# Block one in one chain, with shared buffers, finer steps and another written-out order

## Time and profile before

| what | us |
|---|---|
| median of 3 runs (lowest, highest) | 1390.18 (1389.88, 1391.13) |
| the profiled execution | 1390.79 |
| its span, first to last instruction | 1388.9 |
| PE busy | 1172.6 |
| DVE, POOL, ACT busy | 725.8, 664.4, 574.2 |

### The profile page before, as it was taken

The page is one execution under the profiler, slowest core; times in us unless marked ns, Lnnn a source line. Parts: engine busy times, 40 slices in busy tenths (PEclk is TensorE's granted clock), DMA queues, the critical chain, the costliest instruction groups (busy, mean ns, idle before and its releaser), DMA issues. The chain is left out here.

```text
span 1388.9 us, 17561 instructions
## 1 busy us (share of the span) xinstructions
PE 1172.6 (84%) x6858; PEld 1027.6 (74%) x6858; DVE 725.8 (52%) x1099; ACT 574.2 (41%) x790; POOL 664.4 (48%) x288
## 2 busy tenths in 40 slices
PE   1999979999758699997999974879999677999864
PEld 0999978898547598997889864768788456887743
DVE  2465475653972456447664486244636622653553
ACT  2452236314542356224531453335457342546622
POOL 2664255524334476335642452568436554734643
PEclk9999999999878899999999987889999887999987
DMA  5553243423232355224432331345324415523420
GB/s 184 171 149 92 67 146 111 118 61 106 66 117 70 120 146 146 82 77 122 136 107 61 91 94 59 106 138 157 109 84 128 135 46 182 154 80 95 148 91 31
DMA packets 84433, 152.17 MB, mean 110 GB/s; under 512 B 10560, under 2 KB 16512, under 8 KB 84224
## 3 DMA queue, kind: packets, MB, share of 16 engines
q1 hardware_dynamic: 84352, 151.06, 36.4%
HBM read 149.99 MB, written 1.05 MB: 109 GB/s over the span
## 5 line engine op out<-in xcount | busy, mean ns | idle before, releaser
L739 POOL TENSOR_TENSOR w_lo<-raw,w_hi 128x1024 fp32r<-128x1024 f32 (+3 forms) x284 | 664.2, 2345 | 702.0 <-ACT w_hi L1156 701.7
L1156 ACT ACTIVATE w_hi<-raw 128x1024 fp32r<-128x1024 f32 (+3 forms) x284 | 287.4, 1017 | 566.3 <-PE bulk L791 446.2
L791 PE MATMUL bulk<-w_hi,hT_hi 128*128 128x512 f32 (+1 forms) x800 | 334.3, 418 | 42.9 <-DVE arena L1627 18.0
L791 PE MATMUL bulk<-w_hi,hT_lo 128*128 128x512 f32 (+1 forms) x800 | 321.8, 402 | 0.0
L791 PE MATMUL bulk<-w_lo,hT_hi 128*128 128x512 f32 (+1 forms) x800 | 321.7, 402 | 0.0
L791 PEld LDWEIGHTS bulk<-w_hi,hT_hi 128*128 128x128 f32 x800 | 157.3, 197 | 81.2 <-DVE arena L1627 21.4
L791 PEld LDWEIGHTS bulk<-w_hi,hT_lo 128*128 128x128 f32 x800 | 156.9, 196 | 34.0
L791 PEld LDWEIGHTS bulk<-w_lo,hT_hi 128*128 128x128 f32 x800 | 157.7, 197 | 29.9 <-issue 0.5
L868 PEld LDWEIGHTS chain<-arena 128*128 128x128 f32 x1440 | 170.2, 192 | 7.8 <-DVE arena L1751 2.6
L868 PE MATMUL chain<-arena 128*128 128x128 f32 x1440 | 174.5, 277 | 0.7
L812 PE MATMUL chain<-cst,arena 128*128 128x128 f32 (+2 forms) x512 | 80.4, 306 | 75.6 <-DVE arena L1936 30.6
(11 more groups left out here) (215 smaller groups left out, 1332.5 us busy)
## 6 DMA issues: line engine op xcount, KB each, us to landing
raw<-in_w_in_dram SPq DMA_DIRECT2D x194, 512.0 KB, 3.6
raw<-in_w_out_dram SPq DMA_DIRECT2D x32, 512.0 KB, 3.6
raw<-in_w_branch_dram SPq DMA_DIRECT2D x16, 512.0 KB, 4.0
raw<-in_w_mem_kv_dram SPq DMA_DIRECT2D x8, 512.0 KB, 3.7
raw<-in_w_merge_up_dram SPq DMA_DIRECT2D x16, 256.0 KB, 2.8
raw<-in_w_in_dram SPq DMA_DIRECT2D x8, 420.0 KB, 3.4
gain<-in_ln_rows_dram SPq DMA_DIRECT2D x4, 512.0 KB, 4.6
gain<-in_gains_dram SPq DMA_DIRECT2D x3, 512.0 KB, 4.4
```

Of the source, the lines that this page charges most:

```text
L739: pool.tensor_tensor(lo_of(p, u)[:, 0:n], raw_of(p, u)[:, 0:n], hi_of(p, u)[:, 0:n].bitcast(F32), ALU.subtract).then_inc(p.done("split"), 1)
L791: m = pe.matmul(dst, a, b[:, k, :], start=(kk == 0 and i == 0), stop=(kk == tot - 1 and i == 2))
L1156: return act.activation(dst, src, func, **more)
```

## The change

- **One chain in block one.** `kxT`, `kinorm`, `rope_i` and `rope_a` move from between the groups to behind group 1; `onorm` is done per group, behind each group, and with one square-and-sum instruction per head and row half (8 a group) in place of 4 wide ones. `memT` moves in front of `kxT` (layer 0). `kT` moves to the last level. Tiles come in another sequence: the gates `g00`, `g01` before `zb0`, `zb1`.
- **Shared buffers.** `sq`, `uu`, `kd`, `st`, `qaT`, `pr`, `pt` become views of others' space. `zb`'s drains wait for PE's `sc(1,1)`; the wait of `iT(0)` for `o(1,1)` goes. `mem_raw` lies at `shared`.
- **Pieces.** Top-k in four steps per query block, taps in three steps of four instructions without waits inside a step.
- **By column half.** `mix_b`, `mix`, `mT` take a half of the columns, both row halves; `o0` and `o1` are issued as units 0, 1 of each, then 2, 3 of each, and only the latter wait for `mT(1)`. (Block two's last two tiles get the same sequence of units.)
- **The start.** hT ahead of all splits; `norm_c` in halves; `gain` and `cwT` behind `gc_b`; three parameters of block two loaded with the gain.
- **The order.** `ORDER` is new in all layers of both blocks. What it gives, decoded, at four places:

The diff, cut:

```diff
 def gdn_chain(g):
...
-           ("dec_c", g, 1), ("kk", g, 1), ("x1", g, 0), ("x1", g, 1), ("kT", g)]
+           ("dec_c", g, 1), ("kk", g, 1), ("x1", g, 0), ("x1", g, 1)]
...
+    return out + [("onorm_a", g), ("onorm", g), ("onorm_c", g)]
+def attention_chain():
+    out = [("kxT",), ("kinorm_a",), ("kinorm",), ("rope_i",)] + [("iT", r) for r in range(R)]
+    out += [("raw", 0, 0), ("raw", 1, 0), ("raw", 1, 1), ("rope_a",)] + [("qT", r) for r in range(R)] + [("kaT",)]
+    out += [("topk", qb, i) for qb in range(R) for i in range(TOPK // 16)]
+    for kv in range(2):
+        out += [("sc", kv, 0), ("sc", kv, 1), ("pT", kv, 0), ("pv", kv, 0), ("pT", kv, 1), ("pv", kv, 1)]
...
 def block_one(l):
-    chain = [("hT", r) for r in range(R)] + ([("cwT",)] if l == 0 else []) + [
-        ("baT",), ("ba_a",), ("ba_b",), ("ba_c",), ("gc",), ("gc_b",)]
+    chain = [("hT", r) for r in range(R)] + [("baT",), ("ba_a",), ("ba_b",), ("ba_c",), ("gc",), ("gc_b",), ("gain",)]
     if l == 0:
-        chain += [("tables_a",), ("tables",), ("tables_c",)]
+        chain += [("cwT",), ("tables_a",), ("tables",), ("tables_c",)]
+    mix = [(step, c) for c in range(2) for step in ("mix_b", "mix", "mT")]
+    memory = [("memT", r) for r in range(R)] if l == 0 else []
+    return {"a": chain + gdn_chain(0) + gdn_chain(1) + memory + attention_chain(), "x": mix}
...
                 def onorm_a(g):
                     for r in range(R):
+                        for j in range(4 * g, 4 * g + 4):
+                            x = od[:, r, j * P:(j + 1) * P]
+                            v.tensor_tensor_reduce(od_sq, x, x, 1.0, 0.0, ALU.mult, ALU.add, so[:, 2, r, j:j + 1]).then_inc(
+                                p.own, 1)
+                            v.wait_ge(*p.last())
...
                 def mix(h):
+                    v.wait_ge(*p.after("vector", "gmul", f"g0{h}"))
+                    for qb in range(R):
+                        v.wait_ge(*p.after("vector", "pv", h, qb))
+                    cols = slice(h * 512, (h + 1) * 512)
+                    TT(g0[:, :, cols], g0[:, :, cols], pq[:, :, cols], ALU.mult).then_inc(p.own, 1)
```

More of the change, by code:

```diff
@@ L104, with ones @@
 NARROW = 72
[L106 to L116, removed]
+def ones(names):
+    out = []
+    for name in names.split():
+        c = int(name[-1]) * 512 if name[-1].isdigit() else 0
+        if name in ("ba", "ki"):
+            col = C_BA + 16 - NARROW if name == "ba" else C_KI
+            out.append((name, nat("w_in", col, NARROW, "vector", ks=[8], lhs="narrow")))
+        elif name[0] == "c":
+            out.append(conv_tiles(int(name[2]))[int(name[1])])
+        elif name[0] == "o":
+            out.append((name, nat("w_out", c, 512, "vector", lhs="mix")))
+        else:
+            at = {"qi": C_QI, "kv": 1024, "qa": 0, "za": C_ZA, "zb": C_ZB, "g0": C_GATE, "g1": C_GATE + 1024}
+            out.append((name, nat("w_in", at[name[:2]] + c, 512, "scalar")))
+    return out
+ONE_TILES = ones("ba c00 c10 c20 qi ki kv qa0 qa1 c01 c11 c21 za0 za1 g00 g01 zb0 zb1 g10 g11 o0 o1")
 H2_TILES = {1: (512, 512), 2: (1024, 512), 0: (0, 512), 3: (1536, 512), 4: (2048, 420)}
@@ L149, in units_of @@
 def units_of(tiles):
-    return [(name, t, k0, nk, k0 == 0, k0 + nk == sum(t["ks"])) for name, t in tiles for k0, nk in tile_units(t["ks"])]
+    out = [(name, t, k0, nk, k0 == 0, k0 + nk == sum(t["ks"])) for name, t in tiles for k0, nk in tile_units(t["ks"])]
+    halves = [x for x in out if x[0] in ("o0", "o1")]
+    halves.sort(key=lambda x: x[2] >= KD // 2)
+    return [x for x in out if x[0] not in ("o0", "o1")] + halves
 UNITS = {"mem": units_of(MEM_TILES), "one": units_of(ONE_TILES), "mid": [], "two": units_of(TWO_TILES)}
@@ L159, in bulk_lanes @@
 def bulk_lanes(sec, l):
-    units, mm, conv, drains = UNITS[sec], [], [], {"scalar": [], "vector": []}
+    units, mm, conv, gates, drains = UNITS[sec], [], [], [], {"scalar": [], "vector": []}
     for n, (name, w, _, _, _, last) in enumerate(units):
@@ L166, in bulk_lanes @@
         if w["lhs"] == "T":
-            conv += [("tap", int(name[1]), int(name[2])), ("conv", int(name[1]), int(name[2]))]
+            at = int(name[1]), int(name[2])
+            conv += [("tap",) + at] + [("tap_on",) + at + (k,) for k in (1, 2)] + [("conv",) + at]
         else:
@@ L170, in bulk_lanes @@
             if w["src"] == "w_in" and w["col"] >= C_GATE:
-                conv.append(("gmul", name))
-    return {"s": [("split", n) for n in range(len(units))], "m": mm, "c": conv, "d": drains["scalar"], "v": drains["vector"]}
+                gates.append(("gmul", name))
+    return {"s": [("split", n) for n in range(len(units))], "m": mm, "c": conv, "w": gates, "d": drains["scalar"], "v": drains["vector"]}
 def gdn_chain(g):
@@ L650, in drained @@
             if w["lhs"] == "T":
-                return o.after("vector", sec, l, "tap", int(name[1]), int(name[2]))
+                return o.after("vector", sec, l, "tap_on", int(name[1]), int(name[2]), 2)
             return o.after(w["drain"], sec, l, DRAIN_STEP[w["drain"]], name)
@@ L767, in mm @@
                         left_ready(w, name)
+                    if w["lhs"] == "mix" and k0 == KD // 2:
+                        pe.wait_ge(*p.after("vector", "mT", 1))
                     pe.wait_ge(*p.after("gpsimd", "split", u))
@@ L824, in hT @@
                     c = take("hT", r)
-                    pe.wait_ge(*p.after("vector", "norm_c"))
+                    pe.wait_ge(*p.after("vector", "norm_c", r))
                     transposes(c, [h_nat[:, r, k * P:(k + 1) * P] for k in range(KD)]).then_inc(p.done("hT"), 1)
@@ L991, in pv, with mT @@
                     m.then_inc(p.done("pv"), 1)
-                def mT(r):
-                    c = take("mT", r)
-                    pe.wait_ge(*p.after("vector", "mix", r))
-                    transposes(c, [g0[:, r, k * P:(k + 1) * P] for k in range(KD)]).then_inc(p.done("mT"), 1)
+                def mT(h):
+                    c = take("mT", h)
+                    pe.wait_ge(*p.after("vector", "mix", h))
+                    transposes(c, [g0[:, r, k * P:(k + 1) * P] for k in range(4 * h, 4 * h + 4) for r in range(R)]).then_inc(
+                        p.done("mT"), 1)
                 def xT(r):
@@ L1000, in xT @@
                     if r == 0:
-                        pe.wait_ge(*(o.after("vector", "two", p.l - 1, "ln") if p.l else o.after("vector", "mid", 0, "norm_c")))
+                        pe.wait_ge(*(o.after("vector", "two", p.l - 1, "ln") if p.l else o.after("vector", "mid", 0, "norm_c", 1)))
                     transposes(c, [xs[:, r, k * P:(k + 1) * P] for k in range(KD)]).then_inc(p.done("xT"), 1)
@@ L1222, in conv_silu @@
                 def conv_silu(w, g):
-                    act.wait_ge(*p.after("vector", "tap", w, g))
+                    act.wait_ge(*p.after("vector", "tap_on", w, g, 2))
                     if (w, g) == (0, 1):
```

227 lines of the change are left out of this document (117 added, 110 removed).

## The result

| | before | changed |
|---|---|---|
| median of 4 runs each, side by side (us) | 1390.66 | 1412.65 |
| lowest to highest | 1389.88 to 1391.69 | 1411.11 to 1414.35 |
| ratio, 95% interval | | 1.0158 [1.0140, 1.0176] |
| span of the profiled execution | 1388.9 | 1411.8 |
| PE busy | 1172.6 | 1192.4 |

What follows compares the result with a forecast made beforehand. The tensor engine, busy 84% of the span, was taken as the bound, so only its waits and lower-clock stretches could move time. Terms -17.5 - 7.5 + 8 + 3 + 8 = -6 took 1390.18 to 1384 us, range 1364 to 1405.

Steps and rivals of the forecast that it cites:

- start: Kernel start: later gain row and convolution weights, hT before splits; first bulk matmul at about 18.1 us, minus 17.5 us.
- between the layers: Step into block one's layer 1: hT copies no longer held behind the gain load, minus 7.5 us (3 to 9).
- block one, layer 0: Block one's first layer: 51.5 us of old losses go, 59.6 come with the single chain, plus 8 us.
- block one, layer 1: Block one's second layer: 54 us of old losses go, 57 come with the single chain, plus 3 us.
- block two, both layers: Block two's new order: MLA's scores without bulk 7.5 us per layer, stick-breaking 2, minus 5.5 guessed; plus 8 for both layers.
- the stick-breaking products: Block two: they come one tile earlier, behind four reductions of `lat_a` that can meet splits, costing 2 us.
- Rival 1: Block one, `x1(1,0)` to `g00`: blocked bulk costs more, up to 45 us lost per layer; 1404 us, chance 0.18.
- The blocked bulk costs more: Slower rival on block one, `x1(1,0)` to `g00`'s first unit: up to 45 us lost per layer; 1404 us, chance 0.18.
- The port: Slower rival, convolution stretch: group 0's `onorm` meets splits on the shared port, 6 us more per layer; 1396 us, chance 0.09.
- The levels lose the clock: Slower rival, block one: levels without bulk run at the lower clock, doubling 28 us per layer; 1440 us, chance 0.03.
- Little is exposed: Faster rival: block one's chain at its lower bound, convolution waits of 4 us, block two at nothing; 1363 us, chance 0.23.
- The taps: Block one's convolution: taps issued in three pieces remove the 7.3 us wait; no wait for a tap over 4 us.

Runs made afterwards that it cites:

- spread_short_topk: Changed kernel with rope and index keys moved earlier, bulk units respread, block two in the old order, and half of top-k's rounds left out: 1381.60 us, ratio 0.9951.
- stats_apart: Changed kernel with one bulk unit moved between the two `stat` steps of one-column products, at three places in the convolution: 1408.52 us, ratio 1.0126.

## Why the prediction was wrong

| term | forecast | marks |
|---|---|---|
| start | -17.5 | -17.4 |
| between the layers | -7.5 | -7.1 |
| block one, layer 0 | +8 | +15.2 |
| block one, layer 1 | +3 | +6.9 |
| block two, both layers | +8 | +25.2 |
| sum | -6 | +22.8 |

**The step that failed** is the one on block two: "MLA's scores now stand with no bulk between: ... 7.5 us lost per layer", less "what is left of the idle time before MLA can shrink: minus 5.5, a guess". Its place was right, and so was its mechanism as far as it went: the waits inside MLA are there, 3.1, 1.8 and 1.2 us where I had 2 to 4. The size was not. The stretch lost 13.1 and 12.4 us. I priced the idle time only (6.4 and 5.9 in the trace) and forgot that this stretch also runs at the lower clock, together with the units behind it (10.9 and 10.5 us busy there, 5.4 and 5.2 lost): I had charged such a term in block one and none here. The last 1.3 us a layer are neither idle time nor clock; chain steps that moved across the marks are my guess for them. And the 5.5 us I set against it for idle time elsewhere in block two were a number without a row: outside MLA its layers changed by 0.3 and -0.6 us. With 12.7 and 0 a layer in place of 7.5 and -3.5 (2 for the stick-breaking products, less 5.5) the term is +25. Two kernels show it: with MLA's neighbours alone put back the median falls by 25.2 us, and block two by the marks shortens by 21.0.

**Block one** is 11 us over, the second part of the miss. The part that I had worked out at most length was right: from `x1(1,0)` to `g00`'s first unit I had 45.1 and 42.2 us lost (38.6 and 35.7, 4.5 for the levels, 2 for the restart); idle time plus half of the time at the lower clock give 45.8 and 41.7. The stretch behind the last level is 50.3 us in layer 1, scalar's drain of `za0` ends it as I said; only the clock in it is 0.69 and not near 0.5. What I had too small is behind it: 5.5 and 6.8 us for attention and the output projection, where 13.2 and 15.0 are lost, 8 of them idle (4.1 for `mT(0)` and 2.6 for the first unit are the main ones) and the rest clock; and in layer 1 the convolution stretch, 15.0 against 8. These sizes are read from the trace; the experiments do not take them apart. My ledger of before was also short, 51.5 and 54 where the same count gives 56.2 and 64.7: I had put the time at the lower clock at 10 us by eye and not summed it.

**What I believed of block one's mechanism fell.** Rival 1 and my own text treat the stretch without bulk as blocked by `rope_a` and `za0`. Unblocked, in two arrangements of the units, the kernel is as slow (1388.2 and 1386.4 beside 1387.5, all with block two of before). My reading is that between group 1's levels and the output projection the chain is nearly as late as PE, in the kernel before too (its chain stretch of 175 us has 31.6 to 33.0 idle), and that what a unit covers in one place it delays or uncovers in the next. Only spread_short_topk tests it, at one place. Taking steps off that chain does count: the column half takes 8 us, moving rope and index keys 10.4 in layer 1, of which the convolution takes 6.6.

**Rivals.** "The blocked bulk costs more" gave the nearest time (1404), by the wrong term: the part that it priced at 45 us a layer lost 45.8 and 41.7 with its levels and restart included, as the forecast had it. That it came close is luck. "The port" did not decide: two of group 0's eight reductions met a split and took 2.08 and 2.53 us instead of 0.29, one product 2.85 instead of 0.69, two small steps of the same `onorm` 2.41 and 2.32 instead of 0.2; that is some 10 us of vector work in the convolution stretch of layer 0, which is nevertheless 1.1 us shorter than before; DVE's busy time fell from 725.8 to 719.3. By the Trainium skill, "SBUF — State Buffer", its part on the shared port pair, the loser blocks for the whole instruction; the 2.53 us agree with a split's 2.36. "The levels lose the clock" is out: the window 687.3 to 728.0 with the levels has a clock of 1.00, and it is idle for 4.6 us, the 4.5 that I had. "Little is exposed" is out by the stretches themselves; its terms also add up to 1361, not to the 1363 I gave.

**The taps** went as foreseen: PE's longest wait in the convolution stretches is 3.7 us, before a `stat` step and not for a tap, where 7.3 stood before. That top-k in pieces does nothing by itself is read from the order, in which no other vector step stands between the pieces; no run tests it.

**Open.** What makes the changed kernel's chain stretch, in spite of the halves, 7.3 us longer than before in layer 1 is settled only in part (rope and index keys are the largest piece); the price of each of `onorm` per group, the order of the gates and the missing units beside the levels wasn't tried alone. Nor is it shown how much of the 12.7 us per layer a filler too short to delay MLA's chain would return.

## What to carry to other kernels

Count the lower clock with every stretch from which bulk work is taken, also the short ones: the whole loss in MLA's stretch, idle time and slow matmuls with the units behind, came to about twice the idle time here. An offset without a row ("something elsewhere will shrink") belongs in the range, not in the sum. And before unblocking a queue, ask how late the serial chain beside it is: units moved onto the chain gave nothing here, while starting the next projection on the first half of its input took 10 us a layer off.

## What the runs showed of the hardware

Thirteen matmuls that nothing reads hold the granted clock at 1.00 through a stretch that had 0.78, and its length stays the same to 0.6 us.

The clock fell around steps of one-column products. Windows of the changed kernel, the two steps of 8 (16 records each) between `qi.2` and `qi.4` in layer 0, and the step behind `c21.4` in layer 1:

```profile
65.60:72.00 6.40, 5.10 (x32) 5.05 (x32) 1.82 (x5) 2.80 (x3) 3.28 (x2) 0.66 0.77 221
641.90:649.00 7.10, 3.39 (x17) 3.39 (x17) 0.61 (x2) 3.89 (x4) 4.31 (x2) 0.69 0.26 74
```

PE was full with bulk matmuls until both. In the first it is busy for 5.1 of 6.4 us and the clock is at 0.66 all the same. The clock fell at 67.7 us, when PE had been 1.85 us in such products and 0.45 idle; the next bulk unit still ran slowly (5.47 us for `qi.4`, where 2.9 is full speed). In stats_apart, with `qi.4` between the two steps, the clock stays at 1.00 through both. In the second window it fell at 644.5, inside a wait of 3.7 us and before the products, so that window says nothing of them. Whether the products or the short idle time brought the fall in the first is not shown.
